# The norms' sums over features as two rounded 32-bit products in place of one plain 32-bit product

## The reference, cut to what matters

```python
def rms_norm(x, g):
    xf = x.astype(jnp.float32)
    y = xf * lax.rsqrt(jnp.mean(xf * xf, -1, keepdims=True) + NORM_EPS)
    return (y * g.astype(jnp.float32)).astype(x.dtype)
...
for layer in range(DEPTH):
    x = x + 0.5 * swiglu(rms_norm_2(x, ffn1_norm[layer]), ...)
    hn = rms_norm_2(x, mix_norm[layer])
    ...
```

## Time and profile before

| | before |
|---|---|
| time, median of 3 runs | 2480.82 us (2479.1 to 2486.64) |
| time of the profiled execution | 2479.59 us |
| its span on the core | 2477.8 us |
| TensorE matmuls busy | 2430.9 us, 98% of the span |
| VectorE busy | 1259.3 us, 51% |
| ScalarE busy | 1027.7 us, 41% |
| GpSimd busy | 1322.4 us, 53% |
| mean granted TensorE clock | 0.997 |

### The profile page before, as it was taken

How to read it: one execution, slowest core, us unless ns; L and a number is a source line. 1 busy time by engine, 2 the same in 40 slices (tenths; PEclk the granted TensorE clock), 3 DMA queues, 4 the chain that set the end, 5 groups by cost and what they waited for, 6 DMA issues and landing times.

```text
span 2477.8 us, 33257 instructions
## 1 busy us (share of the span) xinstructions
PE 2430.9 (98%) x13271; PEld 2023.9 (82%) x13271; DVE 1259.3 (51%) x2236; ACT 1027.7 (41%) x1658; POOL 1322.4 (53%) x1010
## 2 busy tenths in 40 slices
PE   8999989999999999999999999999999999999999
PEld 7899868876688888887688888888888888888887
DVE  5677445255585543556573535562525543644443
ACT  4433443346563343436653434542524322533331
POOL 4233345321257776633176767576766545667673
PEclk9999999999999999999999999999999999999999
DMA  4223103210133332322133232333232332232322
GB/s 140 68 69 95 44 18 120 86 52 18 52 110 103 102 102 88 100 66 74 49 99 106 86 119 81 106 98 106 86 114 84 109 102 93 78 119 85 119 85 85
DMA packets 215876, 217.79 MB, mean 88 GB/s; under 512 B 10615, under 2 KB 213106, under 8 KB 215722
## 3 DMA queue, kind: packets, MB, share of 16 engines
q1 hardware_dynamic: 215520, 215.61, 27.5%
q10 hardware_dynamic: 202, 0.06, 0.0%
HBM read 213.53 MB, written 2.12 MB: 87 GB/s over the span
## 4 chain that ended last, share of the span: by engine, by line
PE 93%; DVE 3%; ACT 2%; issue 1%; POOL 0%; DMA 0%; SPq 0%; DVEq 0%; ACTq 0%; POOLq 0%
PE ps L682 58%; PE ps L556 10%; PE ps L675 6%; PE ps L558 5%; PE ps L685 4%; PE ps L679 2%; PE ps L1038 1%; PE ps L1075 1%; PE ps L1057 1%; ACT wh L637 1%; PE ps L2346 1%; PE ps L2407 1%; PE ps L1847 1%; PE ps L704 0%; PE ps L2212 0%
## 5 line engine op out<-in xcount | busy, mean ns | idle before, releaser
L656 POOL TENSOR_TENSOR wl<-raw,wh 128x512 fp32r<-128x512 f32 (+1 forms) x650 | 859.7, 1354 | 1063.5 <-ACT wh L637 1050.0
L682 PE MATMUL ps<-N,wh 128*128 128x512 f32 x2208 | 683.5, 391 | 0.0
L637 ACT ACTIVATE wh<-raw 128x2048 fp32r<-128x2048 f32 (+5 forms) x182 | 311.2, 1710 | 417.4 <-PE ps L682 327.6
L682 PEld LDWEIGHTS ps<-N,wh 128*128 128x128 f32 x2208 | 410.5, 187 | 89.6 <-issue 2.9
L682 PE MATMUL ps<-N,wl 128*128 128x512 f32 (+1 forms) x1104 | 429.8, 389 | 0.0
L682 PE MATMUL ps<-GH,wh 128*128 128x512 f32 x824 | 323.1, 392 | 0.0
L682 PE MATMUL ps<-GH,wl 128*128 128x512 f32 x824 | 320.7, 389 | 0.0
L682 PE MATMUL ps<-GL,wh 128*128 128x512 f32 x824 | 320.6, 389 | 0.0
L682 PEld LDWEIGHTS ps<-N,wl 128*128 128x128 f32 (+1 forms) x1104 | 206.6, 187 | 44.0
L1313 DVE SCALAR_TENSOR_TENSOR H<-ps,H 128x512 f32<-128x512 f32 x96 | 66.4, 691 | 298.6 <-PE ps L682 298.5
L682 PEld LDWEIGHTS ps<-GH,wh 128*128 128x128 f32 x824 | 154.7, 188 | 32.8 <-issue 1.0
(11 more groups left out here) (468 smaller groups left out, 4763.5 us busy)
## 6 DMA issues: line engine op xcount, KB each, us to landing
raw<-in_ffn_w_gate SPq DMA_DIRECT2D x44, 1024.0 KB, 5.3
raw<-in_ffn_w_up SPq DMA_DIRECT2D x44, 1024.0 KB, 5.3
raw<-in_ffn_w_down SPq DMA_DIRECT2D x32, 1024.0 KB, 5.1
raw<-in_w_in_ab SPq DMA_DIRECT2D x15, 1024.0 KB, 5.4
raw<-in_w_in_cd SPq DMA_DIRECT2D x14, 1024.0 KB, 5.0
raw<-in_ffn_w_down SPq DMA_DIRECT2D x16, 768.0 KB, 4.8
raw<-in_c_w_in SPq DMA_DIRECT2D x12, 1024.0 KB, 5.1
raw<-in_w_out_ab SPq DMA_DIRECT2D x8, 512.0 KB, 3.4
```

The source lines that it names most:

```text
L637: nc.scalar.activation(wh[:, b % 2, 0:k, 0:w], raw[:, b % 2, 0:k, 0:w], ACT.Copy).then_inc(S("weights_high"), 1)
L656: nc.gpsimd.tensor_tensor(wl[:, b % 2, ks, 0:w], raw[:, b % 2, ks, 0:w], wh[:, b % 2, ks, 0:w].bitcast(F32), ALU.subtract).then_inc(S("wei ...
L682: last = nc.tensor.matmul(ps[0:m1 - m0, bank, 0:SEQ], w[:, s, k, m0:m1], x(k), start=start, stop=stop)
```

## The change

In place of one plain 32-bit product of `rstd` (or `both`) with the matrix of minus ones, the kernel makes two fp32r products, of a high and a low half. ScalarE copies `rstd` into an fp32r tile `sum_high`, VectorE subtracts it from `rstd` into `sum_low`, and TensorE waits for that subtraction where it waited for the last addition. The matrix of minus ones is copied once into an fp32r tile. The narrow products of ab and cd stay plain. `sum_high` and `sum_low` lie where `tmp` does, `both_high` and `both_low` where `sg` does.

```diff
@@ late_pair_act (and after the squares of ab)
             late_square(act, name, KT - 2)
             late_square(act, name, KT - 1)
+            late_parts_act(act, name)
@@
+    def late_parts_act(act, name):
+        w = T if name in ("ab", "cd") else SEQ
+        act.wait_ge(S("square_added"), tiles_before[name][1] + KT)
+        nc.scalar.activation(sum_high[:, 0:w], rstd[:, 0:w], ACT.Copy).then_inc(S("sum_high"), 1)
+        if name == "ffn0":
+            nc.scalar.activation(both_high[:, :], both[:, :], ACT.Copy).then_inc(S("sum_high"), 1)
+
+    def late_parts_dve(dve, name):
+        w = T if name in ("ab", "cd") else SEQ
+        n = sums_before(name)
+        if name == "ab":
+            nc.vector.tensor_copy(minus_r0[:, :], const("minus_one"))
+        dve.wait_ge(S("sum_high"), n + 1)
+        nc.vector.tensor_tensor(sum_low[:, 0:w], rstd[:, 0:w], sum_high[:, 0:w].bitcast(F32), ALU.subtract).then_inc(S("sum_low"), 1)
+        if name == "ffn0":
+            dve.wait_ge(S("sum_high"), n + 2)
+            nc.vector.tensor_tensor(both_low[:, :], both[:, :], both_high[:, :].bitcast(F32), ALU.subtract).then_inc(S("sum_low"), 1)
@@ late_sum_pe
-        pe.wait_ge(S("square_added"), tiles_before[name][1] + KT)
+        pe.wait_ge(S("sum_low"), sums_before(name) + (2 if name == "ffn0" else 1))
...
-                last = nc.tensor.matmul(ps[:, 4 + h, 0:T // 2], const("minus_one"), rstd[:, h * (T // 2):(h + 1) * (T // 2)], start=True, stop=True)
+                for x, part in enumerate((sum_high, sum_low)):
+                    last = nc.tensor.matmul(ps[:, 4 + h, 0:T // 2], minus_r0[:, :], part[:, h * (T // 2):(h + 1) * (T // 2)], start=x == 0, stop=x == 1)
...
-            last = nc.tensor.matmul(ps[:, 4, :], const("minus_one"), rstd[:, 0:SEQ], start=True, stop=True)
+            for x, part in enumerate((sum_high, sum_low)):
+                last = nc.tensor.matmul(ps[:, 4, :], minus_r0[:, :], part[:, 0:SEQ], start=x == 0, stop=x == 1)
@@ ffn_dve, out_tail_dve and the start of ab
             late_add(dve, ..., KT - 1)
+            late_parts_dve(dve, ...)
```

More of the change, by code:

```diff
@@ L290, in program @@
     rtok = at("rtok", 27304, [P, NT + 1])
+    minus_r0 = at("minus_r0", 25472, [P, P], F32R)
+    sum_high, sum_low = at("sum_high", 26248, [P, T], F32R), at("sum_low", 26776, [P, T], F32R)
+    both_high, both_low = at("both_high", 28016, [P, SEQ], F32R), at("both_low", 28528, [P, SEQ], F32R)
     S0, GA, GB = 27312, 44760, 48984
@@ L812, in late_add, with sums_before @@
             nc.vector.tensor_copy(rstd[:, 0:w], late_square_at(name, 0)).then_inc(S("square_added"), 1)
+    def late_parts_act(act, name):
[14 more added lines that the diff above has]
+            nc.vector.tensor_tensor(both_low[:, :], both[:, :], both_high[:, :].bitcast(F32), ALU.subtract).then_inc(S("sum_low"), 1)
+    def sums_before(name):
+        return LATE.index(name) + (LATE.index(name) > LATE.index("ffn0"))
     def late_sum_pe(pe, name):
-        i = tiles_before[name][0]
-        pe.wait_ge(S("square_added"), tiles_before[name][1] + KT)
+        pe.wait_ge(S("sum_low"), sums_before(name) + (2 if name == "ffn0" else 1))
         if name in ("ab", "cd"):
@@ L822, in late_sum_pe @@
             for h in range(2):
-                last = nc.tensor.matmul(ps[:, 4 + h, 0:T // 2], const("minus_one"), rstd[:, h * (T // 2):(h + 1) * (T // 2)], start=True, stop=True)
+                for x, part in enumerate((sum_high, sum_low)):
+                    last = nc.tensor.matmul(ps[:, 4 + h, 0:T // 2], minus_r0[:, :], part[:, h * (T // 2):(h + 1) * (T // 2)], start=x == 0, stop=x == 1)
         else:
             if name == "ffn0":
-                nc.tensor.matmul(ps[:, 5, :], const("minus_one"), both[:, :], start=True, stop=True)
-            last = nc.tensor.matmul(ps[:, 4, :], const("minus_one"), rstd[:, 0:SEQ], start=True, stop=True)
+                for x, part in enumerate((both_high, both_low)):
+                    nc.tensor.matmul(ps[:, 5, :], minus_r0[:, :], part[:, :], start=x == 0, stop=x == 1)
+            for x, part in enumerate((sum_high, sum_low)):
+                last = nc.tensor.matmul(ps[:, 4, :], minus_r0[:, :], part[:, 0:SEQ], start=x == 0, stop=x == 1)
         last.then_inc(S("norm_summed"), 1)
@@ L1322, in ffn_dve @@
                 late_add(dve, AFTER[f], KT - 1)
+                late_parts_dve(dve, AFTER[f])
     def ffn_pe(pe, f):
@@ L2585, in out_tail_dve @@
         late_add(dve, after, KT - 1)
+        late_parts_dve(dve, after)
     def out_tail_act(act, b0, after):
@@ L2679, in _ @@
             late_square(act, "ab", m)
+        late_parts_act(act, "ab")
         for b in range(2):
@@ L2730, in _ @@
             late_add(dve, "ab", m)
+        late_parts_dve(dve, "ab")
         dve.wait_ge(S("gain_done"), 1)
```

## The result

| | before | changed |
|---|---|---|
| median | 2479.96 us (4 runs) | 2496.12 us (4 runs, 2495.16 to 2500.69) |
| ratio | | 1.0062, 95% interval 1.005 to 1.0074 |
| span of the profiled execution | 2477.8 us | 2494.8 us |
| mean granted TensorE clock | 0.997 | 0.993 |

The changed kernel is slower by 16 us, 0.6%. The forecast was 2491 with 2485.5 to 2495: the direction was right, the time lies just outside the range. Executions of one kernel differ, and with them the clock: of 17 executions of the kernel before, taken beside the experiments, the shortest took 2478.3 at a mean granted clock of 0.997, the longest 2485.8 at 0.993.

What follows compares the result with a forecast made beforehand. TensorE's own stream was taken to bound the kernel; savings of 0.40 a sum against new waits for copy and subtraction summed to +10.5 us on 2480.8, rounded to 2491, range 2485.5 to 2495.

Steps and rivals of the forecast that it cites:

- What bounds the kernel, and that each sum's wait is time lost one for one: Whole kernel: TensorE holds 93% of the chain; a new wait ahead of it is lost time unless it already waited.
- The saving of 0.40 for each 512-column product: At each sum: plain product 0.86, two fp32r products 0.46, so 0.40 less; nine times makes 3.6 us.
- 1.43 from the last addition to TensorE with GpSimd still: Ahead of each sum: copy 0.63, hand-overs 0.07, subtraction 0.68, hand-over to TensorE 0.05; the cost from below.
- The subtraction beside GpSimd: It waits for GpSimd's piece: 0.42 more at cd, 0.73 mla, 0.13 ffn1, 1.17 each at ffn2, conv, ffn3.
- ffn0: Sum gains 0.3, but ScalarE's put-off `bf` delay the first S block's low pieces: +1.1 for ffn0 as a whole.
- The sum: All places added: -0.4 + 1.15 + 1.15 + 1.1 + 6.45 + 1.1 = +10.5 us.
- more than the sum: Put-off queues stall TensorE at ffn1 to ffn3's S blocks, or full GpSimd pieces everywhere: 2492 to 2495; chance 0.12.

Runs made afterwards that it cites:

- plain product: Changed kernel with the halves still made and waited for, but the sum made as the plain 32-bit product of before: 2498.05 us (ratio 1.0066).
- copies between: Changed kernel with ScalarE's copies in the four feed-forward norms moved from ahead of the eight scaled copies to between them: 2497.72 us (ratio 1.0061).
- two norms: Kernel before with the change at ffn2 and conv alone, the other six norms as before: 2490.3 us (ratio 1.0033).

## Why the prediction was right and wrong, point by point

- *What bounds the kernel, and that each sum's wait is time lost one for one*: right. The steps stand at the sums, and no more than 0.3 us came back further on (near 500 us).
- *The saving of 0.40 for each 512-column product*: right (0.40 at ab, 0.43 at ffn3 by the plain product, 0.38 from the rows of the dense stream).
- *1.43 from the last addition to TensorE with GpSimd still*: right. With the total in PSUM the subtraction takes 0.69, TensorE starts 1.41 after the last addition, and the step is 0.96 where 0.98 was said.
- *The subtraction beside GpSimd*: right in kind, and the run with the PSUM operand shows it by taking it away: same instruction, same GpSimd work, 0.69 in place of 1.68. The Trainium skill (SBUF — State Buffer, "Who interferes with whom") says so of two SBUF inputs beside a GpSimd instruction that reads SBUF, and the trace agrees. The size was 0.1 to 0.2 too large: 1.68 in all at ffn2, conv and ffn3, where 0.68 + 1.17 = 1.85 was said, 1.29 at mla (1.41 said), 1.00 at cd (1.10) and 0.69 at ffn1 (0.81). The term gave the subtraction its full 0.68 behind the end of the piece. At all these places it ended 0.54 to 0.57 after the piece, as the row on which the term rested had it too (0.55, rows 5), so some 0.13 of it falls inside the piece's recorded time.
- *ffn0*: right in size (1.18 for 1.1) and place. The copies began at 710.95 and ScalarE's scaled copies stood behind them; TensorE waited 0.51 for GpSimd at the up block and again at the first S block. Moving the copies took both away.
- *The sum*: the step that failed is the sum over places itself, which took every wait at its own length and priced TensorE's clock at nothing. The range did so too: no case in it had the clock. Of the 17 us of the trace about 7 are stretches at the lower clock, 3.3 of them right behind the two sums with a 2.3 us wait. Against the prediction's 10.5 the trace has 7.3 more by the clock and 0.8 less at the sums. That the long waits have a part in it is shown by counting over the five traces with waits of 2.3 or more ahead of a sum of the second block (changed kernel twice, plain product, copies between, two norms): 15 such waits, 10 with the lower clock behind them. In the same traces and the two with the PSUM total there are 14 waits of 0.6 to 1.5 at such sums, none with it. The two kernels with the change at ffn2 and conv alone, which differ in where the total lies and by it in the length of the two waits, 2.39 and 1.37, have it behind both and behind neither. The waits' length is not all: ten of the eleven long waits at ffn1, ffn2 and conv have it behind them, none of the four at ffn3, and why ffn3 is spared isn't shown.
- *The rival "more than the sum"* looked for the excess at the S blocks of ffn1 to ffn3 or in full pieces. Neither came.

What stays open is the other 4 us, the stretches at 58, 546 and 1136. They stand behind waits that both kernels have (at 546 TensorE waits 1.56 and 0.84 for ScalarE, in both). The two traces of before do not have them, both of the changed kernel do, a kernel that is the one before up to ffn2 has two of the three, and the kernel before with its sums later has the one at 546. So they don't need the change ahead of them. Why both traces of the changed kernel show all three isn't shown; that it reaches these places a microsecond or two later is only a guess.

## What to carry to other kernels

A cheaper product is no gain if its operand has to be prepared behind the last thing that TensorE already waits for: here 0.40 us saved stood against 1.4 to 2.4 us of new latency, at six sums of eight. Price such a chain hand-over by hand-over, look where the other engine is when a two-operand VectorE instruction comes up, and then move the consumer behind other work, as far as what waits for its result allows (it paid at ffn1, ffn2, conv and ffn3, came out even at mla, and cost 1.6 us at cd). And where TensorE's new wait is about as long as those here, 2.3 us, add to the range that its clock may fall behind it.

## What the runs showed of the hardware that I had not expected

- The granted clock fell to its lower level behind 10 of 15 waits of 2.3 to 2.8 us in an otherwise dense TensorE stream, for 3.4 us each time, which cost about 1.65 us; behind 14 waits of up to 1.5 us ahead of these sums it never did, though elsewhere it fell behind waits of 1.56 and 0.84 in a row (at 546). Where it fell, a wait of 2.3 us cost nearly 4.
- The same wait at the same place does or doesn't bring it down from one kernel to the next (2.29 at ffn2: yes in the changed kernel, no with the plain product), but the two traces of the changed kernel agreed on all of it. The two of the kernel before differ by one stretch, at 16.1 us, and two kernels with the same instructions up to ffn2 by six.
- Coming 0.12 us later against GpSimd's pieces made a VectorE instruction end 1.2 us later against them, since it met the next piece (ffn1 with the copies between: wait 2.76 in place of 1.51).
